# One inference step of a hybrid decoder layer: another opening (x on two queues, squares added in pairs, ones multiplied between TensorE's sums, one activation table, first weights behind x)

## What is computed

```python
h = rms_norm(x, attn_norm)     # x * rsqrt(mean(x*x) + 1e-6) * g
z = h @ w_in                   # one projection that feeds all branches
mem_k, mem_v = split(rms_norm(mem_prompt, mem_norm) @ w_mem_kv)
```

## Time and profile before

| | |
|---|---|
| median of 3 runs | 1582.35 us |
| profiled execution, first to last instruction | 1583.9 us |
| TensorE busy | 1513.4 us, 96% |
| VectorE, ScalarE, GpSimd busy | 50%, 26%, 6% |
| chain that ended last | PE 92%, ACT 2%, issue 2%, DVE 2% |

### The profile page before, as it was taken

How to read it: one execution, slowest core, us unless ns; L and a number is a source line. 1 busy time by engine, 2 the same in 40 slices (tenths; PEclk the granted TensorE clock), 3 DMA queues, 4 the chain that set the end, 5 groups by cost and what they waited for, 6 DMA issues and landing times.

```text
span 1583.9 us, 31308 instructions
## 1 busy us (share of the span) xinstructions
PE 1513.4 (96%) x13038; PEld 1174.0 (74%) x13038; DVE 799.8 (50%) x1612; ACT 419.0 (26%) x840; POOL 102.8 (6%) x186
## 2 busy tenths in 40 slices
PE   6999999999999989999999988999999999999997
PEld 5888478877777666777566755888788888888885
DVE  4554105522322225521677342777766666666663
ACT  3112145112222222411677553111221111111002
POOL 0000000010100002210400111000000000000000
PEclk9999999999999999999999999999999999999998
DMA  5222353320111126543600387342222222222321
GB/s 218 80 82 78 126 189 102 102 76 29 43 43 33 34 83 176 177 139 104 201 2 2 102 286 270 129 137 93 80 80 80 85 88 80 80 80 93 88 86 57
DMA packets 57897, 162.95 MB, mean 103 GB/s; under 512 B 7296, under 2 KB 20704, under 8 KB 56576
## 3 DMA queue, kind: packets, MB, share of 16 engines
q1 hardware_dynamic: 49184, 121.92, 24.5%
q0 software_dynamic: 7136, 35.73, 6.7%
q10 hardware_dynamic: 1440, 3.33, 0.6%
HBM read 142.96 MB, written 22.15 MB: 104 GB/s over the span
## 4 chain that ended last, share of the span: by engine, by line
PE 92%; ACT 2%; issue 2%; DVE 2%; SPq 1%; DMA 1%; ACTq 0%; DVEq 0%
PE acc L941 25%; PE acc L1040 18%; PE acc L1711 5%; PE acc L1739 5%; PE acc L1720 5%; PE acc L1764 3%; PE acc L1026 2%; PE acc L1135 2%; PE acc L1476 2%; PE acc L1389 2%; PE acc L1500 2%; PE acc L1014 2%; PE acc L1489 2%; PE acc L1149 1%; PE acc L972 1%
## 5 line engine op out<-in xcount | busy, mean ns | idle before, releaser
L1040 PE MATMUL acc<-sb_work,sb_ring 128*128 128x272 f32 x1280 | 334.3, 404 | 1.0 <-ACT sb_work L1896 1.0
L1040 PEld LDWEIGHTS acc<-sb_work,sb_ring 128*128 128x128 f32 x1280 | 231.9, 190 | 55.8 <-issue 8.7
L941 PE MATMUL acc<-sb_work,sb_ring 128*128 128x272 f32 x762 | 186.4, 392 | 0.0
L941 PEld LDWEIGHTS acc<-sb_work,sb_ring 128*128 128x128 f32 x762 | 144.8, 190 | 29.8
L941 PE MATMUL acc<-sb_work 128*128 128x272 f32 x610 | 153.0, 393 | 0.0
L941 PEld LDWEIGHTS acc<-sb_work 128*128 128x128 f32 x610 | 115.7, 190 | 24.6 <-issue 0.8
L2176 ACT ACTIVATE sb_omemT<-acc 128x272 f32<-128x272 f32 x74 | 29.3, 396 | 386.1 <-PE acc L1711 234.8
L2393 DVE TENSOR_TENSOR sb_work<-acc,sb_cst 128x384 f32<-128x384 f32 (+1 forms) x41 | 22.6, 552 | 128.7 <-PE acc L1135 128.7
L1711 PE MATMUL acc<-sb_work,sb_ring 128*128 128x272 f32 x308 | 77.2, 393 | 1.0 <-issue 1.0
L1720 PE MATMUL acc<-sb_work,sb_ring 128*128 128x272 f32 x308 | 77.1, 392 | 0.0
L1896 ACT ACTIVATE sb_work<-acc 128x272 f32<-128x272 f32 x80 | 31.5, 394 | 162.3 <-PE acc L1040 154.6
(11 more groups left out here) (458 smaller groups left out, 2405.2 us busy)
## 6 DMA issues: line engine op xcount, KB each, us to landing
sb_ring<-w_stream SPq DMA_DIRECT2D x144, 512.0 KB, 3.6
sb_work<-pages SPq DMA_DIRECT2D x64, 192.0 KB, 4.0
branch_gates<-sb_work SPq DMA_DIRECT2D x24, 272.0 KB, 4.5
sb_work<-branch_gates POOLq DMA_DIRECT2D x8, 816.0 KB, 19.5
sb_ring<-w_stream SPq DMA_DIRECT2D x16, 384.0 KB, 3.1
sb_work<-mem_kT SPq DMA_DIRECT2D x8, 512.0 KB, 5.9
sb_work<-mem_v SPq DMA_DIRECT2D x8, 512.0 KB, 5.3
query_features<-sb_work SPq DMA_DIRECT2D x10, 272.0 KB, 4.5
```

Of the source, the lines that this page charges most:

```text
L941: mm = pe.matmul(out, w[:, q, :], x[q], start=q == 0, stop=q == n - 1)
L1040: mm = pe.matmul(acc[3][:, half, 0:HALF_T], fill_w[0][:, k, :], hT[:, k, half * HALF_T:(half + 1) * HALF_T], start=k == 0, stop=k == KT - 1)
```

## The change

x and the first two weight tiles go on SyncE's queue and ScalarE's queue: the odd tiles of x on SyncE's, followed at once by weight tiles 0 and 1; the even ones on ScalarE's. Weight tiles 2 to 4 still wait for `x_in[1]`. `mem_xT` moves to GpSimd's queue, behind its wait and ahead of `lora_w`. ScalarE loads one table set that holds Ln and Exp right after its DMA issues. `h_square` gets eight buffers (in rows of `rwT` that are written later) and its wait on TensorE goes. VectorE adds the squares of a pair of tiles, and TensorE sums four pairs instead of eight tiles. TensorE multiplies ones by ones into a bank that is not in use: 18 matmuls of 128 columns ahead of the first pair, 2 after each of the first three pairs, 8 after the last. In unit 0 phase 4 runs ahead of phase 3. The squares of the memory tokens move into ScalarE's unit 1. Counts of semaphores are renumbered to match.

```diff
-        h_square = region(scan0 + PAIRS * T, 2, T)
-        mem_square = region(None, KT, MEM_T)
+        h_square = rwT[:, 0:KT]
+        mem_square = region(scan0 + PAIRS * T, KT, MEM_T)
...
@@ sync
+            for k in range(1, KT, 2):
+                sp.dma_start(xT[:, k, :], A["x_T"][:, k, :]).then_inc(x_in[k // 4], 16)
+            for s in range(2):
+                load(s, s)
             sp.wait_ge(x_in[1], 16 * KT // 2)
-            stream(0, S_IN + RING)
+            for s in range(2, RING):
+                load(s, s)
+            stream(RING, S_IN + RING)
@@ gpsimd
             pool.wait_ge(x_in[1], 16 * KT // 2)
+            pool.dma_start(mem_xT, A["mem_T"]).then_inc(x_in[2], 16)
             pool.dma_start(lw_w, A["lora_w"]).then_inc(rw_in, 16)
@@ tensor
+            def keep_clock(n):
+                for _ in range(n):
+                    pe.matmul(acc[0][:, 0, 0:P], ones_h, ones_h, start=True, stop=True)
+
             pe.wait_ge(means, 1)
-            for k in range(KT):
-                pe.wait_ge(h_squared, k + 1)
+            keep_clock(18)
+            for q in range(KT // 2):
+                pe.wait_ge(rw_x, q + 1)
                 for b in range(2):
-                    mm = pe.matmul(acc[3][:, b, 0:HALF_T], ones_h, h_square[:, k % 2, b * HALF_T:(b + 1) * HALF_T],
-                                   start=k == 0, stop=k == KT - 1)
+                    mm = pe.matmul(acc[3][:, b, 0:HALF_T], ones_h, h_square[:, 2 * q, b * HALF_T:(b + 1) * HALF_T],
+                                   start=q == 0, stop=q == KT // 2 - 1)
                 mm.then_inc(h_sum, 1)
+                keep_clock(2 if q < KT // 2 - 1 else 8)
@@ rw_unit, u == 0
-                    pe.wait_ge(rw_x, 2)
+                    pe.wait_ge(rw_x, X_SUMS + 1)
+                    run(bank(u, 4), s1, [h_sums0[:, 0, q] for q in range(KT // 2)]).then_inc(rw_mm, 1)
+                    pe.wait_ge(rw_x, X_SUMS + 2)
@@ scalar
             act.dma_start(vec[:], A["vectors"]).then_inc(x_in[0], 16)
-            for k in range(KT):
+            for k in range(0, KT, 2):
                 act.dma_start(xT[:, k, :], A["x_T"][:, k, :]).then_inc(x_in[k // 4], 16)
-            act.dma_start(mem_xT, A["mem_T"]).then_inc(x_in[2], 16)
+            act.preload_act_table_set("natural_log_exp_and_others")
...
-                if k >= 2:
-                    act.wait_ge(h_sum, k - 1)
-                act.activation(h_square[:, k % 2, :], xT[:, k, :], ACT.Square).then_inc(h_squared, 1)
-            act.wait_ge(h_sum, KT)
+                act.activation(h_square[:, k, :], xT[:, k, :], ACT.Square).then_inc(h_squared, 1)
+            act.wait_ge(h_sum, KT // 2)
...
-            act.wait_ge(x_in[2], 16)
-            for k in range(KT):
-                act.activation(mem_square[:, k, :], mem_xT[:, k, :], ACT.Square).then_inc(h_squared, 1)
...
                 rw_keep(u, 1)
+                if u == 1:
+                    act.wait_ge(x_in[2], 16)
+                    for k in range(KT):
+                        act.activation(mem_square[:, k, :], mem_xT[:, k, :], ACT.Square).then_inc(h_squared, 1)
@@ vector
+            for q in range(KT // 2):
+                dve.wait_ge(h_squared, 2 * q + 2)
+                dve.tensor_tensor(h_square[:, 2 * q, :], h_square[:, 2 * q, :], h_square[:, 2 * q + 1, :], ALU.add).then_inc(rw_x, 1)
             rw_weights(0)
             dve.wait_ge(x_in[1], 16 * KT // 2)
             dve.wait_ge(h_rms, 1)
```

More of the change, by code:

```diff
@@ L559, in program @@
         N_PAIR = N_RW // 2
-        R_MM, R_KEPT, R_OUT, R_WS, R_X = 6 * N_PAIR, 2 * N_PAIR, 5 * N_PAIR, 2 * N_PAIR, 4
+        X_SUMS = KT // 2
+        MEM_SUM = KT // 2
+        R_MM, R_KEPT, R_OUT, R_WS, R_X = 6 * N_PAIR, 2 * N_PAIR, 5 * N_PAIR, 2 * N_PAIR, KT // 2 + 4
         unit_mm, unit_kept, unit_out, w_summed, x_summed = h_sum, h_rms, hT_ready, mixed, means
-        U_MM, U_KEPT, U_OUT, W_SUM, X_SUM = KT + 3, 2, 2 * KT, N_RW + 1, 3
+        U_MM, U_KEPT, U_OUT, W_SUM, X_SUM = MEM_SUM + 3, 2, 2 * KT, N_RW + 1, 3
         OUT0 = KT - 2
@@ L975, in rw_unit @@
                 mm.then_inc(rw_mm, 1)
-                if u:
+                if u == 0:
+                    pe.wait_ge(rw_x, X_SUMS + 3)
+                else:
                     pe.wait_ge(rw_out, 5 * u - 1)
[L978 to L981, removed]
+                    run(bank(u, 4), s1, [h_sums0[:, 0, q] for q in range(KT // 2)]).then_inc(rw_mm, 1)
                     pe.wait_ge(rw_out, 5 * u)
@@ L984, in rw_unit @@
                 if u == 0:
-                    pe.wait_ge(rw_x, 4)
+                    pe.wait_ge(rw_x, X_SUMS + 4)
                 pe.wait_ge(rw_kept, 2 * u + 1)
@@ L1850, in rw_keep @@
                     act.wait_ge(rw_out, 5 * (u - 1))
-                act.wait_ge(rw_mm, 6 * u + (1, 5)[x])
+                act.wait_ge(rw_mm, 6 * u + (1, 5 if u else 4)[x])
                 act.activation(kept0[:, u % 2, x], bank(u, (0, 4)[x]), ACT.Copy).then_inc(rw_kept, 1)
@@ L1864, in _ @@
                 rw_keep(u, 1)
+                if u == 1:
+                    act.wait_ge(x_in[2], 16)
+                    for k in range(KT):
+                        act.activation(mem_square[:, k, :], mem_xT[:, k, :], ACT.Square).then_inc(h_squared, 1)
                 if u == N_PAIR - 2:
-                    act.wait_ge(h_sum, KT + 1)
+                    act.wait_ge(h_sum, MEM_SUM + 1)
                     own(act.activation(mem_scale, acc[3][:, 0, 0:MEM_T], ACT.Ln, scale=1.0 / D, bias=stat[:, 20:21]))
@@ L1869, in _ @@
             rw_tiles(N_PAIR - 1)
-            act.wait_ge(h_sum, KT + 2)
+            act.wait_ge(h_sum, MEM_SUM + 2)
             act.activation(h2(gates_sT[0:36]), acc[2][0:36, :, 0:HALF_T], ACT.Sigmoid).then_inc(mem_done, 1)
@@ L1880, in _ @@
                    .then_inc(mem_done, 1)
-            act.wait_ge(h_sum, KT + 3)
+            act.wait_ge(h_sum, MEM_SUM + 3)
             act.activation(gates_tm[:, 0:QT, :], acc[2][:, 1, HALF_T:HALF_T + 36 * QT].rearrange("p (n c) -> p n c", n=QT), ACT.Copy)\
@@ L2269, in _ @@
             dve.tensor_tensor(h_sums0[:, 0], hT[:, 0::2, HI], hT[:, 0::2, LO], ALU.subtract).then_inc(rw_x, 1)
-            dve.wait_ge(rw_x, 1)
+            dve.wait_ge(rw_x, X_SUMS + 1)
             dve.tensor_tensor(h_sums0[:, 1], hT[:, 1::2, HI], h_sums0[:, 0], ALU.subtract).then_inc(rw_x, 1)
             dve.tensor_tensor(h_diff0, hT[:, 1::2, HI], hT[:, 0::2, HI], ALU.subtract).then_inc(rw_x, 1)
-            dve.wait_ge(rw_x, 2)
+            dve.wait_ge(rw_x, X_SUMS + 2)
             dve.tensor_tensor(h_sums0[:, 2], hT[:, 1::2, LO], h_sums0[:, 1], ALU.subtract).then_inc(rw_x, 1)
@@ L2300, in _ @@
                     rw_mix(u - 1)
-                dve.wait_ge(rw_mm, 6 * u + 4)
+                dve.wait_ge(rw_mm, 6 * u + (4 if u else 5))
                 dve.tensor_tensor(shared0, bank(u, 3), kept0[:, u % 2, 0], ALU.add).then_inc(rw_out, 1)
```

## The result

The changed kernel has a median of 1570.5 us against 1582.35, a ratio of 0.9929 (95% interval 0.9908 to 0.9950), over seven runs of each; when it was measured again on another occasion the median was 1571.9 and the ratio 0.9945 (0.9918 to 0.9972). One of the eleven runs of that occasion took 3890.7 us, counts as slow and is left out of the ratio. So it is faster by 0.3% to 0.9%. The forecast was 1572.6 in a range of 1570.0 to 1577.0, and faster. That it came out there is in part luck: the opening gave less than I had worked out, and in the traces a place far from it, which I had not thought of, gave some us more. The page first, its line of engines and the line of its instruction queue (packets, MB, share of the 16 DMA engines).

What follows compares the result with a forecast made beforehand. TensorE, busy 96%, bounds the kernel, so only its idle or slow time can be won; the steady state starting at 22.7 instead of 32.40 us saves 9.7, giving 1572.6 us, range 1570.0 to 1577.0.

Steps and rivals of the forecast that it cites:

- The sum behind it: Whole kernel: steady state begins at 22.7 instead of 32.40 us, 9.7 us less, giving 1572.6 us.
- all that follows moves by as much: Behind the opening: bringing phase 3 of unit 0 forward from 32.40 us moves all later work equally.
- x on two queues: Opening loads: issuing in 2.0 instead of 3.98 us; x's first half in at 6.6, second at 9.6 us.
- late bound of 10.34: Landing of x's second half: latest time taken, no change from before because the DMA engines decide.
- Rival 1: Opening: x arrives no earlier (10.34 us); gain 9.1 us, 1573.3 us; chance 10 to 15% not split, given as 15%.
- From the landing on: Opening behind x: squares end at 11.9, hT starts at 15.7, steady state begins at 22.7 us.
- The table: ScalarE's opening: one load while waiting for x, free; Ln's load worth 0, Exp's worth 1.28 us.
- The ones: TensorE's opening: 18 matmuls from 1.4 to 8.6 us cost nothing; the last eight bridge the 3.79 us gap.
- Rival 5: TensorE's opening: ones never bring the full rate; 1 to 2 us slower, 1583.5 to 1584.5 us; 3%.
- No gap above 1 us: TensorE's opening: the change would leave no idle gap longer than 1 us in which the clock could fall.
- Weights in time: Opening: weight tiles 0 and 1 land by 11 to 12.5 us; VectorE's weights done 0.2 us ahead of the norm.
- 2.7 for the clock in unit 0: Unit 0, from hT's start to steady state: full clock worth 2.7 us, 9.17 falling to 7.0.

Runs made afterwards that it cites:

- the padding: Semaphore increments nobody waits for, ahead of TensorE's work: 95 in the kernel before, 1584.2 us (1.0013); 127 in the changed kernel without ones, 1581.4 us (0.9987).
- the experiment: The changed kernel without the load of one table set ahead; 1569.5 us in a single run.

## Why the prediction was right, and where it was not

- **Faster, 1572.6, within the range:** the measured 1570.5 and 1571.9 agree. The sum behind it was 9.7 us, all in the opening. The opening gave 7.8 in the first trace and 8.6 in the second. Split by the first traces: the last square ends 5.7 us sooner (19.14, now 13.40), hT starts 0.3 nearer to it, and the steady state 1.8 nearer to hT. The medians differ by 11.9 and 8.9. What is beyond the opening, 4.1 and 0.3, is hardly more than the noise of the times (3.3 and 4.3 us either way); the traces put 5.3 to 7.4 us of it in the stretch from 4500 to 6200, where the padding shows the positions of TensorE's instructions to be the cause. No step and no rival of mine named them: I took it for granted that all that follows moves by as much and keeps its length. For the sum this was luck, since it stood in for what the opening lacked.
- **x on two queues:** this was the term that was mis-sized. I took 9.6 for the landing; it was 11.1 and 10.4. My late bound of 10.34 was too early by up to 0.8: two weight tiles cost x more than the memory tokens had. Rival 1 (x no earlier) is what happened, and its reason stands: one queue did as well. The first half came at 7.7 and 6.8 instead of 6.6. Of the 1.9 us that the first trace's opening lacks, the landing is 1.5.
- **From the landing on** the working held: squares 2.29 behind it (2.3), hT 3.81 behind the squares (3.8), steady state 7.13 behind hT (7.0), of which 0.14 is the start of TensorE behind VectorE. Another 0.24 was lost in the comparison itself: a phase that starts from rest takes 2.07, and I held its start against one in full flow.
- **The table:** 1.28 for Exp and none for Ln, right; the first load, which I called hidden in the experiment's working, costs 0.5 where it is not done ahead.
- **The ones:** 18 took 6.31 us, 0.21 us an instruction at first where I had 0.25, and were out of the way 2 us ahead of the first pair, which came late. Rival 5 (never fast) is out. "No gap above 1 us" was wrong: 2.1 us lie between the 18 and the first pair, and the granted clock stayed at 1.00. That the eight at the end bridge a gap in which the clock would fall was my reading of the earlier trace rows; without them the gap was 2.5 us in both traces and the clock stayed at 1.00, while it fell in the 3.0 us behind late weights, which the eight did not bridge. The Trainium skill (TensorE: Matmul & The Clock Gate, HAM oscillation) warns that idle gaps of TensorE bring the lower clock back; the gaps of 3.8 us before and of 3.0 us here agree.
- **Weights in time:** tile 1 landed at 12.5 and 11.8, within what I gave; they were done 0.4 ahead of the norm (0.2 expected). The memory tokens' squares and `rw_out` 3 cost nothing, as worked out.
- **2.7 for the clock in unit 0:** from hT to steady state it took 9.17 in the chain before and 7.13 now, 7.37 with the 0.24 above: 1.8. My own figures beside the 2.7 (9.17 and 7.0) make only 2.2; the 2.7 was a slip, and the total of 9.7 did not use it.

## What to carry to other kernels

When a change adds or takes away instructions on an engine with a long unrolled stream, compare the stages far behind it as well: here a hundred of them moved 5 to 7 us in the middle in the traces, and 3 to 9 us in the times of the padded kernels, where the whole opening gave 8, and a reader of medians alone would have thanked the clock for it. Test such an engine's filler against padding that does nothing, and time the padding too. And behind a transfer that is awaited, what stands next in any queue took its share of the DMA engines here (x whole at 10.1 to 11.2 instead of 9.3); moving issues between queues did not help.

## What the runs showed of the hardware that was not expected

TensorE stops for 0.4 to 3.9 us at places of its stream that lie a multiple of 256 instructions apart, whatever the work, and goes on 2.2 to 3.6 us behind the start of a packet of 256 instructions; shifting the stream by 95 to 127 instructions makes two to four such stops vanish in dense small matmuls (87 us against 92 to 94). The Trainium skill (Runtime: NRT & Kernel Launch, Instruction fetch mechanics) describes blocks of 256 instructions fetched ahead and calls the cost of crossing one mostly hidden; the block size agrees with 26,640 instructions in 104 packets, and most of the 103 crossings are hidden here too, but the 5 to 16 that are not cost 7 to 19 us a trace. Semaphore increments back to back on TensorE took 0.153 us each, against 0.051 in their own rows. And a float32 matmul of 128 columns took 0.43 us before the clock rose against 0.26 behind it, less than double.
